# Copies for the pair with added lows in another order on ScalarE, and the reads of the four product banks in one sequence

## The reference, cut to what matters

```
def swiglu(h, w_gate, w_up, w_down):
    return (jax.nn.silu(h @ w_gate) * (h @ w_up)) @ w_down

for i in range(DEPTH):                      # DEPTH = 2
    ...
    h = rmsnorm(x, ffn_norm[i])             # 256 x 2048
    x = x + swiglu(h, ffn_w_gate[i], ffn_w_up[i], ffn_w_down[i])   # 2048 x 5632, 2048 x 5632, 5632 x 2048
```

## Time and profile before

| | |
|---|---|
| median of 3 runs | 2141.0 us (2138.68 to 2141.08) |
| the profiled execution | 2140.9 us, its span 2139.1 us |
| TensorE busy | 2094.4 us, 98% |
| VectorE busy | 1723.5 us, 81% |
| ScalarE busy | 1450.6 us, 68% |
| GpSimd busy | 100.0 us, 5% |
| granted TensorE clock, mean | 0.997 of full |
| moved by DMA | 463.67 MB, mean 217 GB/s |

### The profile page before, as it was taken

The page is one execution under the profiler, slowest core; times in us unless marked ns, Lnnn a source line. Parts: engine busy times, 40 slices in busy tenths (PEclk is TensorE's granted clock), DMA queues, the critical chain, the costliest instruction groups (busy, mean ns, idle before and its releaser), DMA issues.

```text
span 2139.1 us, 28693 instructions
## 1 busy us (share of the span) xinstructions
PE 2094.4 (98%) x9673; PEld 1718.6 (80%) x9673; DVE 1723.5 (81%) x2297; ACT 1450.6 (68%) x1972; POOL 100.0 (5%) x79
## 2 busy tenths in 40 slices
PE   9999999999999999999999999999999999999999
PEld 8888887777777778888888888887777777788887
DVE  5775568898899898889767676787889988898888
ACT  6676657677777777656657676665777777677655
POOL 1101000000000000000011001000000000000000
PEclk9999999999999999999999999999999999999999
DMA  8776457777877786665667777776787788776664
GB/s 278 225 214 201 165 183 216 228 227 228 240 231 231 213 228 200 207 215 178 212 197 246 227 240 232 238 210 196 221 225 234 224 236 236 226 218 201 202 202 141
DMA packets 340216, 463.67 MB, mean 217 GB/s; under 512 B 134576, under 2 KB 137360, under 8 KB 340112
## 3 DMA queue, kind: packets, MB, share of 16 engines
q1 hardware_dynamic: 333936, 441.31, 65.8%
q0 software_dynamic: 6080, 20.99, 5.1%
q10 hardware_dynamic: 96, 0.03, 0.0%
HBM read 408.27 MB, written 2.10 MB: 192 GB/s over the span
## 4 chain that ended last, share of the span: by engine, by line
PE 66%; issue 13%; DVE 9%; ACT 6%; DMA 6%; DVEq 1%; ACTq 0%; POOLq 0%
PE acc L2048 12%; PE acc L2050 12%; PE acc L2049 12%; PE work L2048 9%; PE work L2050 9%; PE work L2049 9%; DMA low_b<-raw 5%; DVE sums L1637 3%; ACT w_hi L1322 3%; DVE sums L1632 3%; DVE w_lo L1619 2%; PE work L2227 1%; ACT low_b L1565 1%; PE work L2265 1%; ACT added_hi L1564 1%
## 5 line engine op out<-in xcount | busy, mean ns | idle before, releaser
L1322 ACT ACTIVATE w_hi<-raw 128x1024 fp32r<-128x1024 f32 x716 | 700.1, 997 | 312.0 <-PE work L2050 201.0
L1619 DVE TENSOR_TENSOR w_lo<-raw,w_hi 128x1024 fp32r<-128x1024 f32 x716 | 816.5, 1147 | 100.2 <-ACT w_hi L1322 99.3
L2048 PE MATMUL work<-w_hi,xT_hi 128*128 128x512 f32 x1236 | 481.0, 389 | 0.0
L2050 PE MATMUL work<-w_hi,xT_lo 128*128 128x512 f32 x1236 | 480.8, 389 | 0.0
L2049 PE MATMUL work<-w_lo,xT_hi 128*128 128x512 f32 x1236 | 480.8, 389 | 0.0
L2048 PE MATMUL acc<-w_hi,xT_hi 128*128 128x512 f32 (+1 forms) x898 | 349.7, 389 | 0.5 <-DVE w_lo L1619 0.5
L2050 PE MATMUL acc<-w_hi,xT_lo 128*128 128x512 f32 (+1 forms) x898 | 346.3, 386 | 0.0
L2049 PE MATMUL acc<-w_lo,xT_hi 128*128 128x512 f32 (+1 forms) x898 | 346.2, 386 | 0.0
L1322 ACT ACTIVATE w_hi<-sums 128x1024 fp32r<-128x1024 f32 x196 | 204.5, 1053 | 192.6 <-DVE sums L1637 132.8
L1619 DVE TENSOR_TENSOR w_lo<-sums,w_hi 128x1024 fp32r<-128x1024 f32 x196 | 239.4, 1222 | 81.5 <-ACT w_hi L1322 81.5
L2050 PEld LDWEIGHTS work<-w_hi,xT_lo 128*128 128x128 f32 x1236 | 232.0, 188 | 48.4
(11 more groups left out here) (203 smaller groups left out, 2449.4 us busy)
## 6 DMA issues: line engine op xcount, KB each, us to landing
raw<-in_ffn_w_down_dram SPq DMA_DIRECT2D x176, 512.0 KB, 4.8
raw<-in_ffn_w_gate_dram SPq DMA_DIRECT2D x160, 512.0 KB, 3.9
raw<-in_ffn_w_up_dram SPq DMA_DIRECT2D x160, 512.0 KB, 5.0
raw<-in_odd_w_in_dram SPq DMA_DIRECT2D x48, 1024.0 KB, 5.8
raw<-in_even_w_in_dram SPq DMA_DIRECT2D x32, 1024.0 KB, 5.8
raw<-in_even_w_out_dram SPq DMA_DIRECT2D x16, 1024.0 KB, 5.0
raw<-in_odd_w_out_dram SPq DMA_DIRECT2D x16, 1024.0 KB, 6.8
low_a<-raw POOLq DMA_DIRECT2D x20, 512.0 KB, 6.4
```

The source lines that it names most:

```text
L1322: act.activation(w_hi[:, s, 0:out], src, ACT.Copy).then_inc(hi_ready, 1)
L1619: dve.tensor_tensor(w_lo[:, s, 0:out], src, w_hi[:, s, 0:out].bitcast(F32), ALU.subtract).then_inc(lo_ready, 1)
L2048: pe.matmul(out_ps, x_hi, wh, start=start, stop=False)
L2050: return pe.matmul(out_ps, x_lo, wh, start=False, stop=stop)
```

## The change

The four copies of pair 0 are ordered anew. At step 18 ScalarE now writes both negated copies and then the high copy of half 0; at step 19 the high copy of half 1. Only the first of the four waits for the load and for TensorE's progress. GpSimd's two transfers follow the negated copies. As the high copies now come behind the semaphore that GpSimd waits for, they get one of their own, `rounded`: TensorE waits for both high copies ahead of each added half. SyncE's load into pair 0's buffer waited for the two added lows alone; now it also waits for the splits, as the other loads do (a split that stands behind the high copies in ScalarE's order). In a layer's first block the four copies follow each other in the same new order. In `JOINS` mix steps 2 and 5 move from step 1 to step 0, behind mix step 1; so VectorE reads the product banks in one sequence, ahead of the low part of sums_a for step 4.

```diff
-JOINS = ((0, (1,)), (1, (2, 5)), (2, (3,)), (3, (4, 6)), (7, (7,)))
+JOINS = ((0, (1, 2, 5)), (2, (3,)), (3, (4, 6)), (7, (7,)))
...
                 def with_up(k):
                     e.x_forms(k)
                     if k == 4:
-                        negate(0, 0)
-                        negate(0, 1)
+                        for step in range(4):
+                            negate(0, step)
...
                         if p in NEGATE and (more or NEGATE[p][0]):
-                            negate(*NEGATE[p])
-                            if NEGATE[p][1]:
+                            k, late = NEGATE[p]
+                            for step in ((0, 1, 2), (3,))[late]:
+                                negate(k, step)
+                            if late:
                                 e.passed()
...
                 if added is not None:
                     for low in low_added:
                         sp.wait_ge(low, n.lows.value(-added, unit=16))
-                else:
-                    sp.wait_ge(lo_ready, n.ring.value(-freed))
+                    sp.nop(nofuse=True)
+                sp.wait_ge(lo_ready, n.ring.value(-freed))
...
-            def negate(k, i):
-
-                n = e.n
+            def negate(k, step):
+
+
+                n, i = e.n, step % 2
                 r = n.raw.slot(2 * RAW, i)
                 assert (r // 2, r % 2) == ((FIRST_SLOT + k) % RAW, i)
-                act.wait_ge(raw_loaded[r // 2], n.raw.turn(2 * RAW, i, plus=1, unit=16))
-                act.wait_ge(up_loaded[n.up.slot(2 * RAW, i) // 2], n.up.turn(2 * RAW, i, plus=1, unit=16))
-                act.wait_ge(half_used, n.half.value(-1))
+                if step == 0:
+                    act.wait_ge(raw_loaded[r // 2], n.raw.turn(2 * RAW, plus=1, unit=16))
+                    act.wait_ge(up_loaded[n.up.slot(2 * RAW) // 2], n.up.turn(2 * RAW, plus=1, unit=16))
+                    act.wait_ge(half_used, n.half.value(-1))
                 src = raw[:, r // 2, i * HALF:(i + 1) * HALF]
-                act.activation(added_hi[:, i, :], src, ACT.Copy)
-                act.activation(added_lo[i][:, :], src, ACT.Copy, scale=-1.0).then_inc(negated, 1)
-                if i:
+                if step < 2:
+                    act.activation(added_lo[i][:, :], src, ACT.Copy, scale=-1.0).then_inc(negated, 1)
+                else:
+                    act.activation(added_hi[:, i, :], src, ACT.Copy).then_inc(rounded, 1)
+                if step == 3:
                     past_pair(n)
...
                 n = e.n
+                pe.wait_ge(rounded, n.lows.value(1, unit=2))
                 pe.wait_ge(low_added[i], n.lows.value(1, unit=16))
```

More of the change, by code:

```diff
@@ L383, in decoder_kernel @@
         down_formed, down_fhi, down_flo = sem("down_formed"), sem("down_fhi"), sem("down_flo")
-        negated, low_added = sem("negated"), [sem(f"low_added{i}") for i in range(2)]
+        negated, rounded, low_added = sem("negated"), sem("rounded"), [sem(f"low_added{i}") for i in range(2)]
         x_summed, form_made, fhi_ready, flo_ready = sem("x_summed"), sem("form_made"), sem("fhi_ready"), sem("flo_ready")
@@ L737, in negate @@
                     e.negate(k, i)
-                    n.negated.c += 1
+                    if i < 2:
+                        n.negated.c += 1
                 def with_up(k):
@@ L1292, in negate @@
             def negate(k, i):
+                if i >= 2:
+                    return
                 pool.wait_ge(negated, e.n.negated.value(1))
```

## The result

The changed kernel takes 2112.91 us in the median of four runs (2112.11 to 2116.41), the one before 2141.04 in four beside it: ratio 0.9872, 95% interval 0.9855 to 0.9889. That is 28.1 us, 1.3% faster, 9 us less than forecast. The profiled execution took 2116.41 us (span 2114.6) and is the slowest of the four, so traces are compared by 2140.9 less 2116.4 = 24.5 us.

What follows compares the result with a forecast made beforehand. TensorE, busy 2094.4 of 2139.1 us, bounds the kernel, with idle time mostly waits for low_b. Savings of 27.8, 5.5, 1.7 and 1.9 us, together 36.9 off 2140.9, gave 2104 us, range 2090 to 2126.

Steps and rivals of the forecast that it cites:

- the gap at step 23: TensorE's wait for the low part of sums_b at step 23; forecast to go, 0.38 us per block.
- the later low part of sums_a: On VectorE, sums_a's low part comes 1.7 us later, at about 506.2 to 507.4, wanted at 508.6.
- VectorE's limit of 41.75: VectorE's stops to exchange sums and copies with ScalarE keep a block at 41.75 us; wait shows at step 6.
- the first rival: DMA queues take turns, half of a load going between low_a and low_b: 2104 to 2113 us, chance 0.15.
- low_a keeps its 6.3 us: low_a's transfer, issued at 493.2, still takes 6.3 us to land: 499.5, against 501.13 when TensorE wants it.
- low_b at 502.8: low_b, issued at 494.1 and served behind low_a, lands near 502.8; TensorE wants it at 503.85 for step 1.
- 16 blocks: Eight blocks in each layer, step 1 to step 1, at 41.75 us for 43.49: 27.8 us saved.
- The starts of the layers: Waits ahead of each layer's first counted block, 5.5 us, and low_a issued one copy earlier at first blocks, 1.9 us.
- The clock: TensorE's lower clock level right after long waits, in 714 to 759 and after 1514.45: 1.7 us saved.
- the second: Rival: more DMA contention, low_b 1 to 1.7 us late in the mean, half the gain: 2113 to 2130, chance 0.10.
- The third: Rival: the load still goes wholly first, low_b lands at 505.8 as before, only 1.9 us left: 2139, chance 0.08.
- The fourth: Rival: low_a, low_b and the load served side by side, low_a lands last at 505.8 before step 0: 2187, chance 0.04.

Runs made afterwards that it cites:

- the last experiment: Changed kernel with pair 2's load held until low_a landed, mix steps 6 and 7 later, one VectorE sum earlier, no work left out: 2082.72 us, ratio 0.9719.

## Why the prediction was right, and where it was not

**What it had right.** The sign, the place and the size in the main: all of the gain is the order of the copies (bank reads as before: 2113.35; alone: 2140.24). low_b is issued at 494.12 (494.1 forecast), its wait fell by 27.6 us, the gap at step 23 is gone, and TensorE's wait on the high copies, SyncE's on the splits and the later low part of sums_a show no cost. VectorE's limit of 41.75 was measured at 41.76 to 41.77 in four kernels, at step 6 above all, with 0.26 us of wait (4.2 us in 16). It is a limit of this order of the work alone; the last experiment keeps the work and reaches 40.8. In the changed kernel itself nothing waits for VectorE: that its blocks take 42.03, so near 41.75, is in part luck, since what is lost at steps 0 and 1 came out a little over what VectorE would have taken. And by the time alone the result, 2112.91, is the first rival's (2104 to 2113), not the forecast's.

**The step that failed: "low_a keeps its 6.3 us".** It takes 8.5 in the median. The copy ends 1 us earlier, but the issue then stands 0.71 us behind the load of pair 2 and not 1.6, and in absolute time low_a lands at 501.7, later than before (494.15 and 6.4: 500.55). The 1 us gained was lost again behind a load, and 1.1 more. That this load is the cause, and not low_b, is shown: low_b cut away, 8.6; low_b later, 8.2; low_a ahead of the load, 5.7; the load held, 4.5. Why the load itself is then served slowly is not: before, it moved 0.40 MB between 495 and 496, after it 0.36, and 0.28 in the next microsecond for 0.35 before, at shares of 93 to 106% in all four. From 496 to 497 its packets took longer (0.970 x 16 / 140 = 0.11 us for 0.935 x 16 / 180 = 0.08). The transposes of words that SyncE issues just ahead (line 1134) may have a part in it; that wasn't tried.

**low_b at 502.8.** By the median it lands at 504.7 (494.12 and 10.6), and that is low_a's lateness passed on: I had put low_b 3.3 us behind low_a, it is 3.05. That includes the sharing with pair 3's load. With this load held it is 2.6 us (9.9 and 0.95, less 8.3), with pair 2's held 2.9, so the turns cost some 0.2 to 0.5 us. My forecast had them at 0 and the first rival at 1.3. The rival's mechanism was the right one there: the Trainium skill ("DMA: Bandwidth & Descriptors", "Queues, rings and completion order") says that an engine goes round its queues packet by packet, and between 500 and 502 the trace agrees, 44 packets to 43 and 41 to 39; in the two microseconds before, 12 to 107, turns alone don't explain it. Its price was too high, as the load's packets are the cheap ones. The wait for low_b stayed small, 0.24 to 0.37 us at step 1 of 15 of the 16 steady blocks and none at the other, since step 0 had itself come late where low_a was, by a wait of up to 1.36 us.

**The sum, term by term**, in the profiled executions:
- 16 blocks: 27.8 forecast, 23.3 measured. The 4.5 us missing are low_a at step 0 and low_b at step 1, less what VectorE's limit would have cost anyway.
- The starts of the layers: 5.5 and 1.9 forecast, nothing measured. low_b's 5.5 us were won for the most part (0.58 us of wait is left in the first layer, none in the second). But low_a's waits grew from 4.7 to 5.7 (its 1.9 were to be saved), one of 1.36 us came at step 0 of the second layer's second block, and the slow stretches of TensorE grew from 8 matmuls (behind 1465.83) to 20, each 0.2 us longer: 2.4 us.
- The clock: 1.7 forecast, for dips that the first term has already. Both, behind 722.18 and behind 1514.45, lie inside the eight blocks whose mean of 43.49 it used. A third, behind 1862.25, lies outside, with a granted clock of 0.61 from 1862 to 1866, and went: from step 1 of the last block to the end it is 276.85 us before and 275.20 after. So some 1.65 us came after all, by luck. No new dip was expected at step 1, and none came; at step 0, in front of which the longest waits now stand, one is new (first layer) and one longer (second).
- Elsewhere 0.5 us were lost: 23.3 + 0 + 1.65 - 0.5 = 24.5.

So 7.4 of the 12.4 us missing lie at two places of the trace, the starts of the two layers, for which the prediction had two lines of its sum, and 4.5 in the steady blocks. At the starts the four copies follow each other directly before they are needed and the loads of pairs 2 and 3 are already out. Holding either load frees both (first blocks of 40.8 to 41.0 us).

**The rivals.** The first and the second both held in part: turns between queues from 500 on, and a landing of low_b 1.9 us later than forecast, most of it for another reason. The third fell (low_b no longer lands with the load). The fourth, low_a behind all the others, didn't come, but it named the tile whose lateness explains most of the difference.

## What to carry to other kernels

An urgent transfer that is issued earlier lands earlier only by what no longer stands ahead of it in the DMA engines: look up which load is issued within a microsecond or two before the new time, and hold that load back if nothing needs it soon. When a wait goes, the next limit may be an engine that is busy 93% of a block; before taking work from it, order its work by who needs it first. And cost the first round of a loop by itself: it has another queue ahead of it than the steady ones.

## What was not expected of the hardware

- The same add of 512 KB lands in 4.5 us with nothing beside it, also 3.1 us behind the issue of a 1 MB load; in 5.7 with the end of the transposes beside it; in 6.4 when issued 1.6 us behind such a load, and in 8.5 when 0.4 to 0.8 us behind. Two adds issued 0.96 us apart, alone, land 4.5 and 6.4 us after their issues.
- From 500 to 502 a load and an add share the engines by packets (44 to 43), and so not by time: 76% to 26%, since an add's packet takes about three times a load's.
- A load can be served at a full share and still slower: 0.56 MB from 496 to 498 at 98.5% with low_b's add cut short; with pair 2's load held, the same queue moves 0.81 MB in the same two microseconds at 104.8%. The cause stays open.
- At the layers' starts the waits of 2.60 and 3.08 us were followed by a lower clock, for 7 and 13 matmuls. Before, of low_a's two waits there the one of 3.12 us (in front of 1465.83) was, for 8 matmuls, and the one of 1.55 (in front of 373.69) was not. The length of the wait isn't all: in the kernel before one of 1.96 us for low_b (in front of 722.18) was followed by a dip, and one of 2.36 (in front of 768.02) was not.
